# Four of the eleven steps of each feed-forward computed in pairs, by seven block products in place of eight, with the loop unrolled

## The chip, the core and the metric

The kernel runs on one core of one Trainium2 chip. TensorE (PE) multiplies and writes its results to PSUM, in eight banks of 128 partitions x 512 float32. VectorE (DVE), ScalarE (ACT) and GpSimd (POOL) work on SBUF, and DVE and ACT also read PSUM. SyncE (SP) issues the transfers of the weights from the chip's memory. Each engine takes its instructions in order, and they wait for one another through semaphores. The metric is the time of one execution in microseconds (us), lower is better, as the median of several runs.

## What is computed

Two blocks of two layers each, for 256 tokens of width 1024 in float32. Each layer has a mixer (an attention, a gated or a recurrent one) between two feed-forwards, so there are eight feed-forwards in all. The change touches only them. This is the function and its use in the first block; the second block has the same two in each layer:

```python
D_MODEL = 1024
SEQ = 256
DEPTH = 2
D_FF = 2816

def _swiglu(x, w1, w3, w2):
    return (jax.nn.silu(x @ w1) * (x @ w3)) @ w2

    for l in range(DEPTH):
        h = _swiglu(x, ffn_w1[l, 0], ffn_w3[l, 0], ffn_w2[l, 0])
        x = _layernorm(ALPHA * x + 0.5 * h, ln_g[l, 0], ln_b[l, 0])
...
        h = _swiglu(x, ffn_w1[l, 1], ffn_w3[l, 1], ffn_w2[l, 1])
        x = _layernorm(ALPHA * x + 0.5 * h, ln_g[l, 2], ln_b[l, 2])
```

## The kernel before

**Split arithmetic.** Each float32 factor is split into a high part, a rounded copy in the type fp32r, and a low part, what is left of it. A product is three matmuls into one bank (`three`, L1908): high x high (L1909), high x the weights' low (L1910), low x the weights' high (L1911). The weights come into one of six slots: slot s has `wf[s]` (the transfer's target, 128 x 2048 float32, 1 MB), `wh[s]` (high) and `wl[s]` (low). Slots 4 and 5 lie in the area `arena`. For each load ACT makes `wh[s]` with `prep(s)` (L618 to L622; from here a *cast*), which waits for the transfer (`ld`) and until PE is done with the slot (`used`). Then DVE makes `wl[s]` with `low(s)` (L1120; from here a *low*), which waits for the cast (`hi`). SP may load `wf[s]` again when the low has been made (`lo`), and it issues its loads in a fixed order, each after that wait.

**A step.** The 2816 hidden columns are worked in eleven steps of 256. The *up* part of a step multiplies the tokens (`xTh`, `xTl`: eight tiles of 128 along the width, two blocks b of 128 tokens) with 256 columns of w1 and 256 of w3 side by side, 512 columns in all, in two units of 1 MB: unit h = 0 has the first 512 rows of the weights, h = 1 the others. The results of the two token blocks are in banks 4 and 5. That is 2 x 8 x 3 = 48 matmuls of 512 columns. ACT takes the silu of the first half of each bank (`silu`, L631), DVE multiplies it with the second (`gated`, L1139, semaphore `h_ready`). PE turns the 256 x 256 hidden values with four small matmuls into bank 6 (`ht_tr`); ACT and DVE split them into `hTh`, `hTl`. The *down* part multiplies them with 256 rows of w2 (1 MB, one slot) into banks 0 to 3, which add up over all steps: 24 matmuls.

**Order.** Everything is written out by hand. Two steps are done in the head (`skewed_head`, L2016; in the first feed-forward `first_head`, L1985), together with the end of what came before. A loop of eight passes follows (L2045 for PE, L716 for ACT, L1297 for DVE, L381 for SP): PE does the up units of a step from slots 0 and 1, the down part of the step before from slot 2, waits for `h_ready` and turns the step's hidden values. The last step lies in the tail. The down part of the last step is in slot 3, which is loaded at the start of the feed-forward; slots 4 and 5 lie unused through the loop. One pass on DVE, and on PE:

```python
                low(0)
                for b in range(TB):
                    ins = gated(b, 4 + b, half)
                ins.then_inc(SEM["h_ready"], 1)
                low(1)
                dve.wait_ge(SEM["ht_hi"], c.next("ht_hi"))
...
                low(2)
```

`settle` (L1126) lets DVE wait for the end of its own last instruction, where the next one reads what that one wrote. The area `y` (128 x 2 x 1024) is free from the head on until the tail.

## Time and profile before

| | |
|---|---|
| runs (us) | 2439.42, 2439.14, 2440.81 |
| median | 2439.42 |
| span of the profiled execution | 2436.0 |
| PE busy | 2394.2 (98%) |
| DVE busy | 1455.7 (60%) |
| ACT busy | 1070.4 (44%) |
| transfers from the chip's memory | 422.49 MB, 174 GB/s over the span |
| mean granted clock of TensorE | 0.996 |

The profiled execution is one run of its own. Its span goes from the first instruction to the last and lies 3.4 us under the median of the runs; what is outside the span is the same for either kernel as far as the profile tells. Matmuls overlap: one lasts 0.39 us in the profile, but the next begins 0.23 us after it, so sums of PE's durations tell less than its starts.

### The profile page before, as it was taken

The numbers are of one execution on the slowest core, as the hardware profiler recorded it, in microseconds if no ns is written. First come the engines' busy times: TensorE is split into PE (matmuls) and PEld (weight loads), VectorE is DVE, ScalarE is ACT, GpSimd is POOL, SyncE is SP. The second block draws the span as 40 slices with busy tenths as digits, with TensorE's granted clock in tenths as the row PEclk, the third lists the DMA queues.
The fourth block names the chain that finished last, engine by engine and source line by source line (L and its number), as shares of the span: only waits on it lengthen the run. The fifth ranks groups of instructions, "written<-read, shape, count | busy, mean of one in ns | idle before, by whom it ended". The sixth has DMA issues, their size and how long they took to land.

```text
span 2436.0 us, 29857 instructions
## 1 busy us (share of the span) xinstructions
PE 2394.2 (98%) x11668; PEld 1978.8 (81%) x11668; DVE 1455.7 (60%) x1599; ACT 1070.4 (44%) x1308; POOL 119.6 (5%) x145
## 2 busy tenths in 40 slices
PE   9999999999999999999999999999999999999998
PEld 8888877888888888788887887798888888777887
DVE  5456867655654666675456456797555545646544
ACT  4443455343343444554344344534434444545442
POOL 0001000000000000000001002102000000200000
PEclk9999999999999999999999999999999999999999
DMA  8566534565655654455564565204556555334552
GB/s 278 187 217 201 189 105 173 191 194 186 206 177 186 210 197 173 139 190 183 188 224 159 187 218 195 91 1 142 194 186 203 187 187 198 121 139 142 186 189 86
DMA packets 281236, 426.58 MB, mean 175 GB/s; under 512 B 11747, under 2 KB 193635, under 8 KB 281136
## 3 DMA queue, kind: packets, MB, share of 16 engines
q1 hardware_dynamic: 273632, 400.04, 49.4%
q0 software_dynamic: 7520, 25.37, 3.4%
q8 instruction: 59, 0.97, 0.2%
q14 instruction: 25, 0.20, 0.0%
HBM read 422.49 MB, written 1.05 MB: 174 GB/s over the span
## 4 chain that ended last, share of the span: by engine, by line
PE 83%; DVE 12%; ACT 2%; issue 1%; POOL 1%; DMA 0%; SPq 0%; DVEq 0%; POOLq 0%; ACTq 0%
PE bank L1909 25%; PE bank L1911 24%; PE bank L1910 24%; DVE wl L1120 4%; PE bank L2366 2%; PE bank L2056 1%; POOL rstd L463 1%; PE bank L1956 1%; DVE stats L1155 1%; DVE arena L1618 1%; DVE y L1222 1%; DVE x L1164 1%; PE bank L2161 1%; DVE y L1189 1%; DVE x L1225 1%
## 5 line engine op out<-in xcount | busy, mean ns | idle before, releaser
L1120 DVE TENSOR_TENSOR wl<-wf,wh 128x2048 fp32r<-128x2048 f32 x355 | 808.6, 2290 | 420.6 <-ACT wh L622 420.1
L1909 PE MATMUL bank<-wh,xTh 128*128 128x512 f32 x2336 | 926.2, 396 | 13.6 <-DVE wl L1120 7.2
L1911 PE MATMUL bank<-wh,xTl 128*128 128x512 f32 x2336 | 910.3, 390 | 0.0
L1910 PE MATMUL bank<-wl,xTh 128*128 128x512 f32 x2336 | 909.1, 389 | 0.0
L622 ACT ACTIVATE wh<-wf 128x2048 fp32r<-128x2048 f32 x355 | 673.3, 1915 | 243.8 <-PE bank L1911 237.8
L1909 PEld LDWEIGHTS bank<-wh,xTh 128*128 128x128 f32 x2336 | 439.6, 188 | 106.7 <-issue 8.7
L1911 PEld LDWEIGHTS bank<-wh,xTl 128*128 128x128 f32 x2336 | 439.1, 188 | 93.2
L1910 PEld LDWEIGHTS bank<-wl,xTh 128*128 128x128 f32 x2336 | 439.9, 188 | 86.5 <-issue 0.7
L1909 PE MATMUL bank<-wh,hTh 128*128 128x512 f32 x704 | 277.4, 394 | 0.2
L1911 PE MATMUL bank<-wh,hTl 128*128 128x512 f32 x704 | 275.0, 391 | 0.0
L1910 PE MATMUL bank<-wl,hTh 128*128 128x512 f32 x704 | 274.6, 390 | 0.0
L631 ACT ACTIVATE sil<-bank 128x256 f32<-128x256 f32 x176 | 60.4, 381 | 297.5 <-PE bank L1911 297.5
L1911 PEld LDWEIGHTS bank<-wh,hTl 128*128 128x128 f32 x704 | 132.4, 188 | 27.9
L1909 PEld LDWEIGHTS bank<-wh,hTh 128*128 128x128 f32 x704 | 132.5, 188 | 27.2 <-DVE wl L1120 0.6
L1910 PEld LDWEIGHTS bank<-wl,hTh 128*128 128x128 f32 x704 | 132.6, 188 | 26.7
L1139 DVE SCALAR_TENSOR_TENSOR hid<-sil,bank 128x256 f32<-128x256 f32 x176 | 68.2, 418 | 124.7 <-ACT sil L631 124.3
L723 ACT ACTIVATE hTh<-bank 128x512 fp32r<-128x512 f32 x64 | 38.3, 598 | 218.7 <-PE bank L2056 218.7
L463 POOL TENSOR_TENSOR rstd<-ve,mhalf 128x1 f32<-128x1 f32 x42 | 35.8, 853 | 1673.4 <-DVE ve L1159 830.0
L1304 DVE TENSOR_TENSOR hTl<-bank,hTh 128x512 fp32r<-128x512 f32 x64 | 44.3, 692 | 110.3 <-ACT hTh L723 110.3
L627 ACT ACTIVATE xTh<-bank 128x512 fp32r<-128x512 f32 x72 | 39.1, 596 | 81.9 <-PE bank L1956 81.5
L2366 PE MATMUL bank<-wf 128*128 128x128 f32 x544 | 65.5, 280 | 3.3 <-DVE wf L1605 2.5
L2366 PEld LDWEIGHTS bank<-wf 128*128 128x128 f32 x544 | 63.0, 195 | 5.6 <-DVE wf L1605 2.9
(333 smaller groups left out, 1512.4 us busy)
## 6 DMA issues: line engine op xcount, KB each, us to landing
wf<-in_ffn_w SPq DMA_DIRECT2D x160, 512.0 KB, 4.8
wf<-in_w_in SPq DMA_DIRECT2D x52, 1024.0 KB, 5.6
wf<-in_ffn_w SPq DMA_DIRECT2D x44, 1024.0 KB, 5.1
wf<-in_ffn_w_down SPq DMA_DIRECT2D x44, 1024.0 KB, 5.1
wf<-in_ffn_w_gate SPq DMA_DIRECT2D x80, 512.0 KB, 4.0
wf<-in_ffn_w_up SPq DMA_DIRECT2D x80, 512.0 KB, 5.0
wf<-in_w_branch SPq DMA_DIRECT2D x16, 1024.0 KB, 5.2
wf<-in_c_w_in SPq DMA_DIRECT2D x14, 1024.0 KB, 6.4
```

Source lines behind the costliest of these rows:

```text
L463: pool.tensor_tensor(dst, src, mhalf[:, 0:n], ALU.pow).then_inc(SEM[to], 1)
L622: act.activation(wh[s], wf[s], ACT.Copy).then_inc(SEM[f"hi{s}"], 1)
L627: act.activation(xTh[:, 4 * r:4 * r + 4, b * P:(b + 1) * P], bank[banks[r]][:, :].rearrange("p (k t) -> p k t", k=4), ACT.Copy).then_inc(S ...
L631: act.activation(sil[:, b, :], bank[bk][:, 0:STEP], ACT.Silu).then_inc(SEM["h_silu"], 1)
L723: act.activation(hTh[0][:, :, :], bank[6][:, :].rearrange("p (k t) -> p k t", k=2), ACT.Copy)\
L1120: dve.tensor_tensor(wl[s], wf[s], wh[s].bitcast(f32), ALU.subtract).then_inc(SEM[f"lo{s}"], 1)
L1139: return dve.scalar_tensor_tensor(hid[:, b, :], sil[:, b, :], half, bank[bk][:, STEP:2 * STEP], ALU.mult, ALU.mult)
L1304: dve.tensor_tensor(hTl[0][:, :, :], bank[6][:, :].rearrange("p (k t) -> p k t", k=2), hTh[0][:, :, :].bitcast(f32), ALU.subtract).then_in ...
L1909: pe.matmul(o, lh, rh, start=start, stop=False)
L1910: pe.matmul(o, lh, rl, start=False, stop=False)
L1911: return pe.matmul(o, ll, rh, start=False, stop=stop)
L2366: ins = pe.matmul(bank[bk][:, i * P:(i + 1) * P], left[:, i, :], right[:, i, :], start=True, stop=True)
```

## The change

Steps 2 to 9, until now the passes of the loop, become two *bodies* of four steps ja, jb, jc, jd written out (2 to 5 and 6 to 9). In each, ja and jb are computed as before. jc and jd are a pair: their two up products are one product of a matrix A (256 tokens x 1024) with B (1024 x 1024), and both are cut into 2 x 2 blocks: A11, A12 are the first token block's two halves along the width, A21, A22 the second's; B11 is jc's first unit, B21 its second, B12 and B22 those of jd. It is computed in Strassen's manner (Winograd's variant) by seven products of 12 matmuls each (`product`) in place of eight.

- **Sums of A**, once in each feed-forward, in body 0: `block_sums` on DVE, ten instructions of 128 x 512, into `wf[5]`, and a cast and a low for slot 5.
- **Sums of B**, once per pair: four subtractions or additions of 128 x 2048 on DVE (`t_made`), in place in `wf[0]`, `wf[1]`, `wf[4]`, `wf[2]`. Three of the seven right factors are loaded blocks, four are such sums; each has a cast and a low of its own (`cast`, `low_of`).
- **Results**: bank 4 (X) goes on adding up through four products; ACT copies it three times on the way (`snapshot`, semaphore `snap`) to quarters of `y`. DVE adds banks 5 (Y) and 7 (Z) to these copies (`block_of`), and silu and gate work from there (`c_silu`, `c_gated`, four of each as before). PE turns the pair's hidden values into banks 6 and 7 (`blocks_hidden`), after the first unit of the next step.
- **Slots**: ja uses slots 3 and 4 in body 0 (0 and 1 in body 1), jb 3 and 1, the pair 4, 1, 3, 2; down parts are in 2, 0, 4 (or 5), 2. The last step's down is now loaded into slot 3 after everything else.
- The loops and what counted in them go; some semaphores are shared. Nothing else of the kernel moves.

```diff
@@ SP, ffn
-            down(w2, STEPS - 1, 3)
-            with c.loop(STEPS - 2, "sp ffn") as j:
-                up(w1, w3, j + 2, 0)
-                down(w2, j + 1)
+            for i in range(BODIES):
+                ja, jb, jc, jd = range(2 + 4 * i, 6 + 4 * i)
+                if i == 0:
+                    up_unit(w1, w3, ja, 3, 0)
+                    up_unit(w1, w3, ja, 4, 1)
+                    down(w2, 1)
+                up_unit(w1, w3, jb, 3, 0)
+                up_unit(w1, w3, jb, 1, 1)
+                down(w2, ja, 0)
+                up_unit(w1, w3, jc, 4, 0)
+                up_unit(w1, w3, jd, 1, 0, "b12_ld")
+                up_unit(w1, w3, jd, 3, 1, "b22_ld")
+                up_unit(w1, w3, jc, 2, 1)
+                sp.wait_ge(SEM["lo3"], c.so_far("lo3"))
+                down(w2, jb, 4)
...
+                up(w1, w3, jd + 1, 0)
+                down(w2, jc, 4 if i < BODIES - 1 else 5)
+                sp.wait_ge(SEM["lo3"], c.so_far("lo3"))
+                down(w2, jd, 2)
+            down(w2, STEPS - 1, 3)
@@ ACT, ffn
-            prep(3)
-            with c.loop(STEPS - 3, "act ffn"):
-                prep(0, 2)
...
+            for i in range(BODIES):
+                if i == 0:
+                    prep(1, 2)
+                    prep(0)
+                    act.wait_ge(SEM["t_made"], c.next("t_made"))
+                    cast(5, wf[5])
+                    prep(3, 2)
+                    act.wait_ge(SEM["used4"], c.so_far("used4"))
+                    silus()
...
+                prep(4, 2)
+                take_both(1)
+                prep(2, 2)
+                act.wait_ge(SEM["t_made"], c.next("t_made", 3))
+                cast(3, wf[4])
+                act.wait_ge(SEM["used1"], c.so_far("used1"))
+                silus()
+                cast(1, wf[1])
+                cast(0, wf[0])
+                take_both(0)
+                snapshot(part_1, 4)
+                prep(4)
...
@@ DVE
+        def block_sums():
...
+            s1, s2, s3, s4 = (sumA[:, j, :, :] for j in range(4))
+            dve.tensor_tensor(s1, A(1, 0, xTh), A(1, 1, xTh), ALU.add)
+            dve.tensor_tensor(s2, A(1, 0, xTl), A(1, 1, xTl), ALU.add)
+            dve.tensor_tensor(s3, A(0, 0, xTh), A(1, 0, xTh), ALU.subtract)
+            settle(dve.tensor_tensor(s4, A(0, 0, xTl), A(1, 0, xTl), ALU.subtract))
+            dve.tensor_tensor(s1, s1, s2, ALU.add)
+            settle(dve.tensor_tensor(s3, s3, s4, ALU.add))
+            settle(dve.tensor_tensor(s2, s1, A(0, 0, xTh), ALU.subtract))
+            settle(dve.tensor_tensor(s2, s2, A(0, 0, xTl), ALU.subtract))
+            settle(dve.tensor_tensor(s4, A(0, 1, xTh), s2, ALU.subtract))
+            dve.tensor_tensor(s4, s4, A(0, 1, xTl), ALU.add).then_inc(SEM["t_made"], 1)
...
+            for i in range(BODIES):
+                if i == 0:
+                    low(1)
+                    low(0)
+                    block_sums()
+                    low(5)
+                    low(3)
+                    both_gated(half)
+                else:
+                    low(3)
+                    take_both(1)
+                    take_both(0, 7)
+                    low(0)
+                    both_gated(half)
+                    low(1)
+                low(4)
+                dve.wait_ge(SEM["b12_ld"], c.next("b12_ld", 32))
+                dve.tensor_tensor(wf[0], wf[1], wf[4], ALU.subtract).then_inc(SEM["t_made"], 1)
+                dve.wait_ge(SEM["b22_ld"], c.next("b22_ld", 32))
+                dve.tensor_tensor(wf[1], wf[3], wf[1], ALU.subtract).then_inc(SEM["t_made"], 1)
+                take_both(1)
+                dve.wait_ge(SEM["t_made"], c.next("t_made", 2))
+                dve.tensor_tensor(wf[4], wf[1], wf[4], ALU.add).then_inc(SEM["t_made"], 1)
+                low(2)
+                dve.wait_ge(SEM["t_made"], c.next("t_made"))
+                dve.tensor_tensor(wf[2], wf[2], wf[4], ALU.subtract).then_inc(SEM["t_made"], 1)
+                low_of(3, wf[4])
+                both_gated(half)
...
@@ PE, ffn
-            with c.loop(STEPS - 3, "pe ffn"):
-                for h in range(2):
-                    whole_unit(h, h, [bank[4][:, :], bank[5][:, :]])
...
+            for i in range(BODIES):
+                if i == 0:
+                    whole_unit(3, 0, outs45)
+                    whole_unit(4, 1, outs45)
+                    both_down(2, 0)
...
+                pe.wait_ge(SEM["h_ready"], c.next("h_ready"))
+                both_hidden()
+                whole_unit(3, 0, outs45)
+                whole_unit(1, 1, outs45)
+                both_down(0, 1)
+                pe.wait_ge(SEM["h_ready"], c.next("h_ready"))
+                both_hidden()
+                product(4, A(0, 0), bankX, True)
+                product(2, A(0, 1), bankY, True)
...
+                product(3, A_sum(SUM2), bankX, False)
+                product(1, A_sum(SUM3), bankZ, True)
...
+                product(0, A_sum(SUM1), bankX, False)
+                both_down(4, 0)
...
+                product(2, A_sum(SUM4), bankX, False)
...
+                product(3, A(1, 1), bankZ, False, "used5" if i == BODIES - 1 else None)
```

How the order stands at the places that matter, by engine. **DVE, from the last low of the head on**, before (the whole pass of the loop; wl0 is the low of slot 0):

```order
L1120 TENSOR_TENSOR wl0<-wf0,wh0 128x2048 [waits hi0]
L1138 ISA
L1139 SCALAR_TENSOR_TENSOR hid<-sil,bank4 128x256 [waits h_silu]
L1138 REGISTER_ALU
L1139 SCALAR_TENSOR_TENSOR hid<-sil,bank5 128x256 [waits h_silu]
L1120 TENSOR_TENSOR wl1<-wf1,wh1 128x2048 [waits hi1]
L1304 TENSOR_TENSOR hTl<-bank6,hTh 128x512 [waits ht_hi]
L1120 TENSOR_TENSOR wl2<-wf2,wh2 128x2048 [waits hi2]
```

and in the changed kernel, body 0, from the low of the second up unit of jb (wl1) to the gate of ja (`hid`); the five rows left out are more sums:

```order
L1177 TENSOR_TENSOR wl1<-wf1,wh1 128x2048 [waits hi1]
L1177 TENSOR_TENSOR wl0<-wf0,wh0 128x2048 [waits hi0]
L1195 TENSOR_TENSOR arena<-xTh 128x512
L1196 TENSOR_TENSOR arena<-xTl 128x512
L1197 TENSOR_TENSOR arena<-xTh 128x512
...
L1203 TENSOR_TENSOR arena<-xTh,arena 128x512 [waits dve]
L1204 TENSOR_TENSOR arena<-arena,xTl 128x512 [waits dve]
L1177 TENSOR_TENSOR wl5_52<-arena,wh5_51 128x2048 [waits hi5]
L1177 TENSOR_TENSOR wl3<-wf3,wh3 128x2048 [waits hi3]
L1233 SCALAR_TENSOR_TENSOR hid<-sil,bank4 128x256 [waits h_silu]
L1233 SCALAR_TENSOR_TENSOR hid<-sil,bank5 128x256 [waits h_silu]
```

Before, one low stands ahead of a step's gate; now two lows, ten sums and two more lows stand ahead of the first one. **ACT at the same place**, before (one pass) and then in the changed kernel:

```order
L620 REGISTER_ALU [waits ld0]
L622 ACTIVATE wh0<-wf0 128x2048 [waits used0]
L631 ACTIVATE sil<-bank4 128x256 [waits used1]
L631 ACTIVATE sil<-bank5 128x256
L622 ACTIVATE wh1<-wf1 128x2048 [waits used1,ld1]
L723 ACTIVATE hTh<-bank6 128x512 [waits ht_tr]
```

```order
L618 ACTIVATE wh1<-wf1 128x2048 [waits used1,ld1]
L618 ACTIVATE wh0<-wf0 128x2048 [waits used0,ld0]
L629 ACTIVATE wh5_51<-arena 128x2048 [waits used5,t_made]
L618 ACTIVATE wh3<-wf3 128x2048 [waits used3,ld3]
L643 ACTIVATE sil<-bank4 128x256 [waits used4]
L643 ACTIVATE sil<-bank5 128x256
L618 ACTIVATE wh4_49<-arena 128x2048 [waits used4,ld4]
```

The silus of ja now stand behind a cast that waits for the sums. **PE in the pair**, the first row of each group of matmuls (each product goes on for eleven more rows):

```order
L2118 MATMUL bank6<-ident,hid 128x128 [waits h_ready]
...
L2141 MATMUL bank4<-wh4_49,xTh 128x512 [waits lo4]
...
L2141 MATMUL bank5<-wh2,xTh 128x512 [waits lo2]
...
L2141 MATMUL bank4<-wh3,wh5_51 128x512 [waits lo3,lo5,snap]
...
L2141 MATMUL bank7<-wh1,wh5_51 128x512 [waits lo1]
...
L2141 MATMUL bank4<-wh0,wh5_51 128x512 [waits lo0,snap]
...
L2049 MATMUL bank0<-wh4_49,hTh 128x512 [waits lo4,ht_ready]
...
L2141 MATMUL bank4<-wh2,wh5_51 128x512 [waits lo2,snap]
...
L2141 MATMUL bank7<-wh3,xTh 128x512 [waits lo3,c_made]
```

and before, where a pass ends and turns its hidden values:

```order
L1909 MATMUL bank3<-wh2,hTh 128x512
L1910 MATMUL bank3<-wl2,hTh 128x512
L1911 MATMUL bank3<-wh2,hTl 128x512
L2053 REGISTER_ALU
L2056 MATMUL bank6<-ident,hid 128x128 [waits h_ready]
L2056 MATMUL bank6<-ident,hid 128x128 x3
```

The wait for `h_ready` stands at the same distance behind the units as before; the pair has one wait for a copy, or for DVE's results, at nearly every product.

## Rows read from the trace of the kernel before

**Rows 1.** The page: busy time of each engine, then the chain by engine.
```profile
PE 2394.2 (98%) x11668; PEld 1978.8 (81%) x11668; DVE 1455.7 (60%) x1599; ACT 1070.4 (44%) x1308; POOL 119.6 (5%) x145
...
PE 83%; DVE 12%; ACT 2%; issue 1%; POOL 1%; DMA 0%; SPq 0%; DVEq 0%; POOLq 0%; ACTq 0%
```

**Rows 2.** PE in order of time (start us, us): matmuls of a head, then two passes' turns.
```profile
486.06 0.39 PE L1910 MATMUL bank<-wl,xTh 128*128 128x512 f32 x1
486.29 0.40 PE L1911 MATMUL bank<-wh,xTl 128*128 128x512 f32 x1
...
607.34 0.60 PE L2056 MATMUL bank<-ident,hid 128*128 128x128 f32 x4
624.13 0.60 PE L2056 MATMUL bank<-ident,hid 128*128 128x128 f32 x4
```

**Rows 3.** The page, groups of instructions: busy us, mean ns of one, idle before.
```profile
L1120 DVE TENSOR_TENSOR wl<-wf,wh 128x2048 fp32r<-128x2048 f32 x355 | 808.6, 2290 | 420.6 <-ACT wh L622 420.1
...
L622 ACT ACTIVATE wh<-wf 128x2048 fp32r<-128x2048 f32 x355 | 673.3, 1915 | 243.8 <-PE bank L1911 237.8
...
L723 ACT ACTIVATE hTh<-bank 128x512 fp32r<-128x512 f32 x64 | 38.3, 598 | 218.7 <-PE bank L2056 218.7
...
L1304 DVE TENSOR_TENSOR hTl<-bank,hTh 128x512 fp32r<-128x512 f32 x64 | 44.3, 692 | 110.3 <-ACT hTh L723 110.3
```

**Rows 4.** Second feed-forward, end of the head: DVE, ACT, PE; then PE's turns (source view).
```profile
486.86 2.29 DVE L1120 TENSOR_TENSOR wl<-wf,wh 128x2048 fp32r<-128x2048 f32 x1 [1.38 <-ACT wh L622]
...
484.91 1.91 ACT L622 ACTIVATE wh<-wf 128x2048 fp32r<-128x2048 f32 x1
490.63 1.91 ACT L622 ACTIVATE wh<-wf 128x2048 fp32r<-128x2048 f32 x1
...
489.93 0.38 PE L1963 MATMUL bank<-ident,hid 128*128 128x128 f32 x2
...
L2056 PE MATMUL bank<-ident,hid x24: 270/272/273, 506.5 to 590.9; 128*128 128x128 f32 x24
```

**Rows 5.** First feed-forward, end of the head: DVE, PE; then PE's turns (source view).
```profile
30.56 0.41 DVE L1139 SCALAR_TENSOR_TENSOR hid<-sil,bank 128x256 f32<-128x256 f32 x1
...
40.58 0.60 PE L1978 MATMUL bank<-ident,hid 128*128 128x128 f32 x4
...
L2056 PE MATMUL bank<-ident,hid x32: 269/272/273, 57.4 to 175.3; 128*128 128x128 f32 x32
```

**Rows 6.** Transfers: issue to landing (page); a full stretch (windows: busy of engines, clock, share, GB/s).
```profile
wf<-in_ffn_w SPq DMA_DIRECT2D x160, 512.0 KB, 4.8
...
16.00:18.00 2.00, 2.00 (x10) 1.65 (x10) 1.60 (x1) 1.64 (x1) 0.00 (x0) 1.00 1.11 357
```

**Rows 7.** DVE on 128 x 512: a group by form, then two in time, the last waiting.
```profile
L1609 DVE TENSOR_TENSOR wf<-wf,ident 128x512 f32<-128x512 f32 x4 | 2.6, 686 | 0.0
...
461.89 1.28 DVE L1155 BATCH_NORM_STATS2 stats<-y 128x6 f32<-128x512 f32 x2
463.33 0.21 DVE L1158 BATCH_NORM_AGGREGATE mv<-stats 128x2 f32<-128x12 f32 x1 [0.16 <-DVE stats L1155]
```

**Rows 8.** A gap of PE: windows (PE, PEld, DVE, ACT, POOL, clock, share, GB/s), and the end.
```profile
1564.00:1565.00 1.00, 0.00 (x0) 0.00 (x0) 1.00 (x3) 0.53 (x2) 0.00 (x0) 1.00 0.00 0
1565.00:1566.00 1.00, 0.28 (x2) 0.28 (x3) 1.00 (x3) 0.00 (x0) 0.00 (x0) 1.00 0.00 0
1566.00:1567.00 1.00, 1.00 (x8) 1.00 (x8) 0.86 (x2) 0.00 (x0) 0.00 (x0) 0.64 0.00 0
1567.00:1568.00 1.00, 1.00 (x7) 1.00 (x7) 0.55 (x1) 0.00 (x0) 0.00 (x0) 0.50 0.00 0
1568.00:1569.00 1.00, 1.00 (x6) 1.00 (x6) 0.14 (x1) 0.00 (x0) 0.00 (x0) 0.50 0.00 0
1569.00:1570.00 1.00, 1.00 (x8) 1.00 (x7) 0.94 (x2) 0.12 (x1) 0.00 (x0) 0.66 0.00 0
...
2430.00:2431.00 1.00, 0.00 (x0) 0.00 (x0) 0.99 (x2) 0.00 (x0) 0.00 (x0) 0.50 0.00 0
```

More of the change, by code:

```diff
@@ L12 @@
 import math
-from contextlib import ExitStack, contextmanager
+from contextlib import ExitStack
 import numpy as np
@@ L210, in program @@
     negm = negm_wide[:, P:T]
+    yq = [y[:, i // 2, (i % 2) * HALF:(i % 2 + 1) * HALF] for i in range(4)]
+    C11, C21, C12, C22 = yq
+    part_v, part_1, part_5 = C21, C12, C22
+    sumA = wf[5].rearrange("p (j k t) -> p j k t", j=4, k=4)
+    sumA_h, sumA_l = (t[5].rearrange("p (j k t) -> p j k t", j=4, k=4) for t in (wh, wl))
+    SUM1, SUM2, SUM3, SUM4 = range(4)
+    bankX, bankY, bankZ = (bank[i][:, :] for i in (4, 5, 7))
     names = []
@@ L342, in _, with load @@
         c = Counts(sp, SEM["held"])
-        def load(s, *pieces):
+        def load(s, *pieces, to=None):
             sp.wait_ge(SEM[f"lo{s}"], c.so_far(f"lo{s}"))
@@ L628, in take_x, with cast, snapshot, c_silu @@
                                bank[banks[r]][:, :].rearrange("p (k t) -> p k t", k=4), ACT.Copy).then_inc(SEM["xt_hi"], 1)
+        def cast(s, src):
+            act.wait_ge(SEM[f"used{s}"], c.so_far(f"used{s}"))
+            c.count(f"used{s}")
+            act.activation(wh[s], src, ACT.Copy).then_inc(SEM[f"hi{s}"], 1)
+        def snapshot(to, s):
+            act.wait_ge(SEM[f"used{s}"], c.so_far(f"used{s}"))
+            act.activation(to, bankX, ACT.Copy).then_inc(SEM["snap"], 1)
+        def c_silu(to, src):
+            act.activation(to[:, 0:STEP], src[:, 0:STEP], ACT.Silu).then_inc(SEM["h_silu"], 1)
+        def silus():
+            for b in range(TB):
+                silu(b, 4 + b)
         def silu(b, bk):
@@ L726, in ffn @@
+            prep(2)
+            take_both(1)
+            take_both(0, 7)
+            prep(3)
             if after:
@@ L1307, in ffn @@
+            low(5)
+            take_both(1)
+            take_both(0, 7)
+            low(2)
+            low(3)
             gated(0, 4, half).then_inc(SEM["h_ready"], 1)
@@ L1979, in both_hidden, with both_down, A, A_sum @@
             ins.then_inc(SEM["ht_tr"], 1)
+        outs45 = [bank[4][:, :], bank[5][:, :]]
+        def both_down(s, i):
+            pe.wait_ge(SEM["ht_ready"], c.next("ht_ready"))
+            pe.wait_ge(SEM[f"lo{s}"], c.next(f"lo{s}"))
+            for b in range(TB):
+                ins = down(s, i, b, (0, 1))
+            ins.then_inc(SEM[f"used{s}"], 1)
+        def A(b, r):
+            t = slice(b * P, (b + 1) * P)
+            return [(xTh[:, 4 * r + q, t], xTl[:, 4 * r + q, t]) for q in range(4)]
+        def A_sum(j):
+            return [(sumA_h[:, j, q, :], sumA_l[:, j, q, :]) for q in range(4)]
+        def product(s, lhs, o, start, freed=None):
+            pe.wait_ge(SEM[f"lo{s}"], c.next(f"lo{s}"))
+            for q, (lh, ll) in enumerate(lhs):
+                r = slice(q * HALF, (q + 1) * HALF)
+                ins = pe.matmul(o, lh, wh[s][:, r], start=start and q == 0, stop=False, skip_group_check=not start)
+                if freed and q == 0:
+                    ins.then_inc(SEM[freed], 1)
+                pe.matmul(o, lh, wl[s][:, r], start=False, stop=False, skip_group_check=not start)
+                ins = pe.matmul(o, ll, wh[s][:, r], start=False, stop=q == 3, skip_group_check=not start)
+            ins.then_inc(SEM[f"used{s}"], 1)
+        def blocks_read():
+            pe.wait_ge(SEM["h_ready"], c.next("h_ready", 3))
+        def blocks_hidden():
+            pe.wait_ge(SEM["h_ready"], c.next("h_ready"))
+            for rows_, bk in (((C11, C21), 6), ((C12, C22), 7)):
+                for k in range(2):
+                    for b in range(TB):
+                        ins = pe.transpose(bank[bk][:, k * T + b * P:k * T + (b + 1) * P], rows_[b][:, k * P:(k + 1) * P],
+                                           ident[:, :])
+                ins.then_inc(SEM["ht_tr"], 1)
         def busy(n, bk, t):
@@ L2061, in ffn @@
+            blocks_read()
+            unit(0, 0, 0, bank[4][:, :])
+            blocks_hidden()
+            unit(1, 1, 0, bank[4][:, :]).then_inc(SEM["up"], 1)
+            both_down(5, 1)
             pe.wait_ge(SEM["ht_ready"], c.next("ht_ready"))
```

214 lines of the change are left out of this document (129 added, 85 removed), and 5 rows, old and new, of the table PER_PASS.

## The prediction

> **What bounds the kernel now.** I read the page first: PE is busy 98% of the span, DVE 60%, ACT 44%, and 83% of the chain that ended last is PE's own work [rows 1]. Then PE in order of time: matmuls of 512 columns start 0.23 us apart and a pass of the loop comes every 16.79 us (607.34 to 624.13) [rows 2]. The second feed-forward has its loop begin at 490.2 (after the head's last two turns at 489.93) and turns its first hidden values at 506.5 [rows 4]: 16.3 us for 72 matmuls, 0.227 us each, so PE has no hole there. Each matmul taken out of a pass is worth 0.227 us, as long as the others keep up. DVE's slack in a pass: three lows of 2.29 and about 1.4 us of small work, 8.3 of 16.8 us. That is an average; where a change piles work in front of one PE wait, the average says nothing. So the sum needs the order on DVE and ACT, walked through with these durations.
>
> **What goes from PE.** A pair needs 84 up matmuls in place of 96. Two pairs in eight feed-forwards: 16 x 12 = 192 matmuls x 0.227 = **43.6 us** less. The down matmuls and the turns are as many as before. The loop cost PE nothing that a row shows (16.79 = 72 x 0.227 + four turns at about 0.11), so its unrolling gives nothing.
>
> **What comes on DVE and ACT, per pair.** DVE: three more lows (seven right factors in place of four units) and four sums of 128 x 2048, at 2.29 each [rows 3] = 16.0, and three `block_of` at 0.69: +18. ACT: three more casts at 1.92 and three copies at 0.60 [rows 3]: +7.6. Over a body of four steps (PE: 4 x 16.8 - 2.7 = 64.4) DVE then needs about 4 x 8.3 + 18 = 51 and ACT about 37. On average both fit.
>
> **What comes on DVE once per feed-forward, in body 0.** Ten sums of 128 x 512. The nearest rows: 0.69 alone, 0.60 from start to start in a row (1.28 for two), and 0.16 of idle before an instruction that waits for the one before it [rows 7]. Five are settled (0.69 + 0.16), four follow freely (0.60), the last takes 0.69: 4.25 + 2.4 + 0.69 = 7.3 us. Bounds: 6.0 (all at 0.60) to 8.5 (all settled). On the wait inside such a chain the Trainium skill ("VectorE: DVE Perf Modes", The DRAIN you can't avoid) says that a semaphore after each instruction costs nothing extra; the 0.16 us of rows 7 speak against it. By its rule the sums would take 10 x 0.69 = 6.9 us and the total 3 us less.
>
> **The place that decides: the first turn of body 0.** PE does ja's two units (48 matmuls) and a down part (24), 16.3 us, then waits for ja's gated values. On DVE that gate stands behind: low of slot 4, low 2, low 1 (jb), low 0 (ja's down part), ten sums, low 5, low 3, in this order; on ACT its silus stand behind cast 5, which waits for the sums, and cast 3. Walk for the second feed-forward, body start at 490.2:
> - SP issues jb's first unit (slot 3) when the head's low of that slot is done, 486.86 + 2.29 = 489.15 (before, slot 0; now the same instruction for slot 3) [rows 4], then slot 1 and slot 0 at once, whose buffers are free. A unit is two transfers, the second is issued 0.4 us after the first and lands 4.8 us later [rows 6]: 489.2 + 5.3 = 494.5. The next megabytes queue behind it; at full rate the stream runs at 357 GB/s [rows 6], some 3.0 us for 1 MB: slot 1 lands at 497.5, slot 0 at 500.5.
> - ACT is done with its head casts at 494.5 (490.63 + 2 x 1.92) [rows 4]. Cast 1 497.5 to 499.4, cast 0 500.5 to 502.5.
> - DVE: low 1 to 501.8, low 0 502.5 to 504.8, sums to 512.1. Cast 5 to 514.1, cast 3 to 516.0, silus to 516.7; low 5 514.1 to 516.4, low 3 to 518.7, two gates (0.41 each, 0.75 the overlapping pair) [rows 5] to 519.4.
> - PE, ready at 506.5, turns at 519.5: **it stands 13.0 us**.
>
> With transfers at no cost DVE alone (lows 4, 2, 1, 0 from 492.6 on, sums, wait for cast 5, lows 5 and 3, gates) still ends at 516.5, so 10 us is the lower bound; loads 1 us later make it 14. The first feed-forward loads earlier: its head's slot-3 low may follow the gate at 30.56 as soon as ACT has made the cast, about 34.6, in place of waiting for PE. PE's body starts at 41.0 (turn at 40.58) and would turn at 57.4 [rows 5]. Slots 3, 1, 0 land at 40.0, 43.0, 46.0; the same walk gives low 1 to 48.3, low 0 to 50.6, sums to 57.9, gates to 65.3: 8.0 us. All others begin like the second. Sum: 7 x 13.0 + 8.0 = **99 us** of PE standing.
>
> **After that.** ACT and DVE come out of it late; the next sums of B, which need jd's second unit in slot 3 (loaded only after the late low 3), push low 3 and the gate of jb to 0.8 us behind PE: 8 x 0.8 = 6. From there on the same walk finds no PE wait: in the pair the copies of X take 0.6 us beside the 2.7 of a product into another bank, each right factor's low is done 2 us or more ahead, and in body 1 DVE stands idle ahead of each gate. The tightest place of body 1 is again jb's gate ahead of the pair: done 1.2 us before PE wants it, behind three loads in a row (b12, b22, B21). I take 0 there; loads 1 us slower, or 2 us of extra DVE work, would make it up to 2 us per feed-forward. The tail has DVE's four pieces (low 5, hidden values, lows 2 and 3) 1 us or more ahead, and slot 5's later load lands 20 us before the next head wants it: 0.
>
> **The clock.** PE does nothing from 1564 to 1565 and for 0.72 us of the next window; in the four windows after that the granted clock is 0.64, 0.50, 0.50, 0.66, and it is 0.50 at 2430 too, where PE has no more work [rows 8]. 0.50 is its lower level, 1.2 GHz. The four windows lose 0.36 + 0.50 + 0.50 + 0.34 = 1.7 us. Each of the eight stops is far longer than that gap (1.7 us by the windows), so I charge 1.7 each; between 0 and 3.4 are the bounds. It takes the place of the 0.8 above (PE is later, DVE is not), so 0.9 more: 8 x 0.9 = **7 us**. The Trainium skill ("TensorE: Matmul & The Clock Gate", What's actually happening) says the same in kind, an idle array falls to 1.2 GHz and comes back when kept busy; rows 8 agree with it.
>
> **The sum.** -43.6 + 99 + 6 + 7 = +69 us on the profiled span: 2436.0 + 69 = 2505. The runs' median is 3.4 us over that span, which the change doesn't touch: **2508 us**.
>
> **Rivals.**
> 1. *All of it is hidden, the product saving stays.* It would need the gate of ja 13 us earlier. The order has no room for that: ja's gate stands behind the sums and two more lows on an engine that doesn't reorder, and behind cast 5 on ACT. 2439.4 - 43.6 = **2396**. Against it every row of the walk; for it only that I may have misread which wait is meant. 3%.
> 2. *The stop is real but short*: the transfers are early, the sums near 6.0, the clock unharmed: 10.0 - 1.3 = 8.7 in seven, 5 in the first, 0.8 behind each: +66 + 6 - 44 = +28 to +45: **2467 to 2485**. For it: the landings are the softest numbers of the walk (a lone unit's landing is measured, a burst's is worked out). Against it: DVE's own chain. 12%. At this end, if the change also gained something in the loop that I don't see (over 28 us, 1.8 per pair), it would be no change; 2% for within 0.2%.
> 3. *The pair is too dense as well*: per body 13 pieces of 2.29 us have to come in the right order, and the seven waits of PE in the pair each catch a late low, or the three loads ahead of it come 1 to 2 us late. 2 to 3 us in each of 16 pairs eats the saving: +32 to +48: **2540 to 2556**. For it: the 1.2 us of slack in body 1. Against it: 13 us of standing lets all that is queued behind catch up, and in body 1 DVE waits for casts, not the other way. 10%.
> 4. *The change doesn't do what it says on PE*: a product that adds up in one bank for twelve matmuls runs slower than a unit that changes banks every three. But the matmuls at 486.06 and 486.29 [rows 2] are from a head's unit that stays in bank 5 for twelve, and they stand 0.23 us apart as well. I give it 1%, inside case 3.
>
> **How the numbers follow.** Forecast (a stop of 11.5 to 14.5 in each body 0, saving as counted, clock 0 to 3.4 each): 72%, 2508, own range 2488 to 2530. Case 2: 12%, case 3: 11%, case 1: 3%, no change: 2%. To hold 8 in 10 the range takes the forecast's own and reaches into both neighbours: 2478 to 2534. A measurement of this kernel can tell about 0.2% (5 us) from no change. Slower by more: 0.72 + 0.12 + 0.11 = 0.95, of which 0.02 go to the other two for what the walk may have overlooked: 0.93; within 0.2%: 0.02 + 0.01 = 0.03; faster: 0.03 + 0.01 = 0.04.
>
> **What the profile after would show.** PE's idle ahead of the first turn of each feed-forward after the head, released by DVE's gate: 12 to 14 us, seven times, and about 8 in the first. The 40 slices would show eight dents of PE, with a lower clock in them. In body 1 and in the pairs, PE matmuls 0.227 us apart with no gap over 1 us. PE starts 192 matmuls fewer. DVE busy up by 16 x 18 + 8 x 9.6 = some 365 us, to about 75% of the span. Wrong would be: a stop under 10 us (then the burst of loads or the sums were mis-sized), gaps inside the pairs (case 3), or no stop at all.

## The result, and the profile after

The changed kernel takes **2501.21 us** (median of four runs, 2500.56 to 2504.1), where the one before takes 2439.47 on the same footing: a ratio of 1.0256, with a 95% interval of 1.0243 to 1.027. The profiled execution has a span of 2502.2 us against 2436.0, so 66.2 us have to be explained. Some 3 of them are scatter: the profiled execution is the slowest of the four (2504.1), the other three took 2500.56 to 2501.22. An execution takes 1.8 to 1.9 us longer than its own span, in both kernels (2504.1 for a span of 2502.2, and 2437.8 for one of 2436.0 in the runs of e1). So of the 3.4 us between span and median, only 1.8 lie outside the span; the rest is the distance of that one execution from the median. The page of the changed kernel (busy times; then PE's busy tenths and the granted clock in 40 slices; the chain by engine; and one of the groups):

```profile
PE 2367.5 (95%) x11476; PEld 1954.6 (78%) x11476; DVE 1789.8 (72%) x1847; ACT 1199.7 (48%) x1412; POOL 120.6 (5%) x145
...
PE   8999999989989999998998999999799899999798
...
PEclk9999999989989999998999999999899899999899
...
PE 73%; DVE 17%; ACT 4%; DMA 3%; issue 2%; POOL 1%; SPq 1%; DVEq 0%; POOLq 0%; ACTq 0%
...
L2118 PE MATMUL bank<-ident,hid 128*128 128x128 f32 x136 | 24.5, 310 | 91.6 <-DVE hid L1233 91.6
```

Beside [rows 1]: PE has 192 matmuls fewer (11668 to 11476), and yet less of the span is its own work, 95% for 98%. PE's slices are dented where they were whole, and so is the clock. In the chain 10 points have gone from PE to the other engines. L2118 is the turn of the hidden values: PE stood 91.6 us ahead of it in all, and DVE's gate (L1233) ended the wait. The waits of PE by line say in how many pieces (us, times, longest):

```profile
PE bank L2118 <- DVE hid L1233: 91.6, 8, 12.7
PE bank L2049 <- DVE wl L1177: 7.4, 13, 1.0
PE bank L2103 <- DVE hid L1233: 7.2, 9, 2.4
```

Eight stops, one in each feed-forward; the next two rows were there before, within 0.2 us. These are PE's rows at three of the eight (start, us, and in brackets the idle time ahead), with the three matmuls behind the second:

```profile
64.71 1.12 PE L2118 MATMUL bank<-ident,hid 128*128 128x128 f32 x4 [6.98 <-DVE hid L1233]
...
522.79 1.12 PE L2118 MATMUL bank<-ident,hid 128*128 128x128 f32 x4 [11.74 <-DVE hid L1233]
523.56 0.78 PE L2049 MATMUL bank<-wh,xTh 128*128 128x512 f32 x1
524.13 0.63 PE L2050 MATMUL bank<-wl,xTh 128*128 128x512 f32 x1
524.56 0.63 PE L2051 MATMUL bank<-wh,xTl 128*128 128x512 f32 x1
...
2356.80 1.12 PE L2118 MATMUL bank<-ident,hid 128*128 128x128 f32 x4 [12.75 <-DVE hid L1233]
```

Matmuls of 512 columns start 0.43 us apart behind a stop, not 0.23 as in [rows 2]: the clock is down. In windows around the second stop (length, then busy of PE, PEld, DVE, ACT, POOL, then the granted clock; the last two columns are the transfers):

```profile
512.00:514.00 2.00, 0.00 (x0) 0.00 (x0) 1.93 (x4) 0.00 (x0) 0.00 (x0) 0.79 0.04 14
514.00:516.00 2.00, 0.00 (x0) 0.00 (x0) 1.54 (x3) 0.36 (x1) 0.00 (x0) 0.50 0.00 0
516.00:522.00 6.00, 0.00 (x0) 0.00 (x0) 4.42 (x3) 5.69 (x5) 0.00 (x0) 0.50 0.00 0
522.00:526.00 4.00, 3.21 (x10) 2.74 (x11) 4.00 (x5) 0.60 (x1) 0.00 (x0) 0.50 0.67 199
526.00:527.00 1.00, 1.00 (x5) 0.76 (x4) 1.00 (x1) 0.00 (x0) 0.00 (x0) 0.60 1.09 366
527.00:530.00 3.00, 3.00 (x15) 2.45 (x14) 2.66 (x3) 0.00 (x0) 0.00 (x0) 1.00 0.99 312
```

From 522.8 to 526 PE works at 0.50, in the next window at 0.60, which is some 2.0 us of work lost. Summed in the same way over all windows of 1 us (PE's busy time times what the clock lacks of 1), the kernel before loses 6.8 us, the changed one 25.0, of which 18.2 lie behind the eight stops (1.5 to 3.0 each). So the 66.2 us are **91.6 (stops) - 43.6 (192 matmuls at 0.227) + 18.2 (clock)**. PE's other waits add up to 1.0 us more than before, so the sum closes to about 1 us.

Why the gate is late can be read from DVE and ACT in the second feed-forward. Its body begins at 494.57 here, by the walk's own measure: 0.27 us after the head's last turns, which are at 494.30 (before, 489.93 and 490.2). ACT's casts of slots 1 and 0 and of the sums, then DVE: the lows of slots 1 and 0, the first and the last sum, the lows of slots 5 and 3, the two gates:

```profile
502.14 1.92 ACT L618 ACTIVATE wh<-wf 128x2048 fp32r<-128x2048 f32 x1 [3.43 <-DMA wf<-in_ffn_w]
504.72 1.92 ACT L618 ACTIVATE wh<-wf 128x2048 fp32r<-128x2048 f32 x1 [0.67 <-DMA wf<-in_ffn_w]
...
515.64 1.91 ACT L629 ACTIVATE wh<-arena 128x2048 fp32r<-128x2048 f32 x1 [8.99 <-DVE arena L1204]
...
504.09 2.29 DVE L1177 TENSOR_TENSOR wl<-wf,wh 128x2048 fp32r<-128x2048 f32 x1 [2.66 <-ACT wh L618]
506.68 2.29 DVE L1177 TENSOR_TENSOR wl<-wf,wh 128x2048 fp32r<-128x2048 f32 x1 [0.29 <-ACT wh L618]
508.88 0.68 DVE L1195 TENSOR_TENSOR arena<-xTh 128x512 f32<-128x512 f32 x1
...
514.19 0.69 DVE L1203 TENSOR_TENSOR arena<-xTh,arena 128x512 f32<-128x512 f32 x1
514.91 0.69 DVE L1204 TENSOR_TENSOR arena<-arena,xTl 128x512 f32<-128x512 f32 x1
517.58 2.29 DVE L1177 TENSOR_TENSOR wl<-arena,wh 128x2048 fp32r<-128x2048 f32 x1 [1.97 <-ACT wh L629]
519.79 2.28 DVE L1177 TENSOR_TENSOR wl<-wf,wh 128x2048 fp32r<-128x2048 f32 x1
521.99 0.74 DVE L1233 SCALAR_TENSOR_TENSOR hid<-sil,bank 128x256 f32<-128x256 f32 x2
```

It is a chain with little idle time in it: a landing, two lows, the sums (508.88 to 515.60), the cast of the sums, two lows, the gates. PE's last matmul before the turn starts at 510.66, and the gates end at 522.73.

### The profile page after: what moved, and what is told of

Read it like the earlier page. It is cut to its first block, busy times and chain, and to the rows that moved or that the text cites. A ratio compares the mean times of both kernels' runs of the same rounds, so it can differ in the third digit from the quotient of the medians.

```text
span 2502.2 us, 27918 instructions
## 1 busy us (share of the span) xinstructions
PE 2367.5 (95%) x11476; PEld 1954.6 (78%) x11476; DVE 1789.8 (72%) x1847; ACT 1199.7 (48%) x1412; POOL 120.6 (5%) x145
## 4 chain that ended last, share of the span: by engine, by line
PE 73%; DVE 17%; ACT 4%; DMA 3%; issue 2%; POOL 1%; SPq 1%; DVEq 0%; POOLq 0%; ACTq 0%
PE bank L2049 17%; PE bank L2051 17%; PE bank L2050 17%; DVE wl L1177 7%; PE bank L2145 4%; PE bank L2141 4%; PE bank L2144 4%; PE bank L2568 2%; ACT wh L618 2%; DMA wf<-in_ffn_w_down 2%; DMA wf<-in_ffn_w 1%; POOL rstd L459 1%; PE bank L2096 1%; PE bank L2118 1%; DVE stats L1249 1%
## 5 line engine op out<-in xcount | busy, mean ns | idle before, releaser
L2049 PE MATMUL bank<-wh,xTh 128*128 128x512 f32 x1824 | 730.5, 401 | 13.9 <-DVE wl L1177 7.4
L2051 PE MATMUL bank<-wh,xTl 128*128 128x512 f32 x1824 | 715.6, 392 | 0.0
L2050 PE MATMUL bank<-wl,xTh 128*128 128x512 f32 x1824 | 715.2, 392 | 0.0
L2049 PEld LDWEIGHTS bank<-wh,xTh 128*128 128x128 f32 x1824 | 347.9, 191 | 89.7 <-issue 9.1
L2051 PEld LDWEIGHTS bank<-wh,xTl 128*128 128x128 f32 x1824 | 346.5, 190 | 73.9
L2050 PEld LDWEIGHTS bank<-wl,xTh 128*128 128x128 f32 x1824 | 347.5, 191 | 68.6 <-issue 0.7
L1177 DVE TENSOR_TENSOR wl<-arena,wh 128x2048 fp32r<-128x2048 f32 x87 | 198.2, 2286 | 51.1 <-ACT wh L618 35.3
L618 ACT ACTIVATE wh<-arena 128x2048 fp32r<-128x2048 f32 x79 | 151.0, 1913 | 38.6 <-PE bank L2051 32.2
L1183 DVE TENSOR_TENSOR wl<-wf,wh 128x2048 fp32r<-128x2048 f32 x64 | 145.0, 2285 | 23.9 <-ACT wh L629 23.9
L2118 PE MATMUL bank<-ident,hid 128*128 128x128 f32 x136 | 24.5, 310 | 91.6 <-DVE hid L1233 91.6
L2144 PE MATMUL bank<-wl,wh 128*128 128x512 f32 x256 | 99.6, 389 | 0.0
L2145 PE MATMUL bank<-wh,wl 128*128 128x512 f32 x256 | 99.6, 389 | 0.0
```

The lines of the kernel that those rows point to most:

```text
L618: act.activation(wh[s], wf[s], ACT.Copy).then_inc(SEM[f"hi{s}"], 1)
L1177: dve.tensor_tensor(wl[s], wf[s], wh[s].bitcast(f32), ALU.subtract).then_inc(SEM[f"lo{s}"], 1)
L1183: dve.tensor_tensor(wl[s], src, wh[s].bitcast(f32), ALU.subtract).then_inc(SEM[f"lo{s}"], 1)
L2049: pe.matmul(o, lh, rh, start=start, stop=False)
L2050: pe.matmul(o, lh, rl, start=False, stop=False)
L2051: return pe.matmul(o, ll, rh, start=False, stop=stop)
```

## The experiments

The theory (A): the stops come from the amount and the order of the work on DVE between the head and the first gate, with the late landings ahead of it; the pairs themselves cost nothing. The rivals: the loss lies in the unrolled code; in the pairs; in the transfers alone; or in the order alone.

### e1: the kernel before with its loops written out

```diff
-            with c.loop(STEPS - 3, "pe ffn"):
+            for j in range(STEPS - 3):
```
(and the same on SP, ACT and DVE)

> The kernel before with its loops in the feed-forwards written out and nothing else changed. Theory (the loss is the stop in body 0, the unrolling is free): 2439 +- 2 us, PE's first turn after the head at the same place as before. Rival (the written-out code itself costs, by instructions that have to be fetched or by lost pacing): clearly above 2439, a good part of the 62 us.

Measured: 2440.11 us, ratio 1.0006 (0.9997 to 1.0015). The unrolling costs nothing that can be told: the interval ends at 0.15%, 3.7 us.

### e2: nine of the ten sums left out

The kernel leaves the sums out to see what they cost; its result isn't that of the product.

```diff
-            dve.tensor_tensor(s1, A(1, 0, xTh), A(1, 1, xTh), ALU.add)
...
-            dve.tensor_tensor(s4, s4, A(0, 1, xTl), ALU.add).then_inc(SEM["t_made"], 1)
+            dve.tensor_tensor(s4, A(0, 1, xTh), A(0, 1, xTl), ALU.add).then_inc(SEM["t_made"], 1)
```

> The changed kernel with one of the ten sums of A left (the other nine are left out, so the sums of A are not those of the product). Theory (DVE's chain ahead of ja's gate sets the stop): the sums take 0.7 us in place of the 6.7 of the profile, the stop falls from 11.5 to about 5.5 us, the total by 8 x 6.0 = 48 to 2453 us. Rival (the landing of the loads or ACT sets it): less than 10 us change.

Measured: 2453.54 us, ratio 1.0062 (1.0047 to 1.0077). PE's waits:

```profile
PE bank L2109 <- DVE hid L1224: 43.8, 9, 6.8
```

The stops shrink by 91.6 - 43.8 = 47.8 us, 6.0 in each feed-forward, and nine sums take 508.88 to 514.91, 6.0 us: the sums stand on PE's path with their whole length. What is left is two lows and a cast too many, and the landings.

### e3: small matmuls in the stop, to hold the clock

```diff
                     both_down(2, 0)
+                    busy(95 if ready else 60, 7, ident[:, :])
```

> The changed kernel with 95 small matmuls (60 in the first feed-forward) of the identity into bank 7 ahead of the first turn of body 0, inside PE's stop: 95 x 0.114 = 10.8 us of 11.5 to 12.7. They change no result. Theory (the lower clock after the stop costs about 2.3 us each, 18 us in all): the granted clock stays at 1.00 and the total falls by 15 to 18 us, to about 2485. Rival (the clock costs nothing since DVE sets the pace then as well; the 18 us are gaps elsewhere): 2501, no change.

Measured: 2558.85 us, ratio 1.0491 (1.0475 to 1.0507). A miss: I had taken 0.114 us for one call, but each float32 matmul of 128 columns leaves two records of PE and takes some 0.22. PE's records of the 95 calls in the second feed-forward (source view: minimum, median, maximum ns, first and last start):

```profile
L2162 PE MATMUL bank<-ident x190: 271/275/276, 516.5 to 537.6; 128*128 128x128 f32 x190
```

21.1 us of filler where the stop had 11.7, so the time says nothing by itself. The account does. The eight runs of filler keep PE for 160.6 us, 69.0 more than the stops, and PE's wait at this turn (L2118) is gone; the clock loses 11.9 us in all, 13.1 less than in the changed kernel. That makes +55.9, and the profiled span is 56.4 longer (2558.6): here the 13.1 us of clock did come out in the time. e8 repeats it with half the number.

### e4: the loads of slots 1 and 0 ahead of slot 3

```diff
+                    up_unit(w1, w3, jb, 1, 1)
+                    down(w2, ja, 0)
+                    up_unit(w1, w3, jb, 3, 0)
+                else:
+                    up_unit(w1, w3, jb, 3, 0)
+                    up_unit(w1, w3, jb, 1, 1)
+                    down(w2, ja, 0)
```

> The changed kernel with the loads of jb's second unit (slot 1) and of ja's down part (slot 0) issued ahead of jb's first unit (slot 3) in body 0, so that they don't wait for the head's low of slot 3. Theory (the burst of three loads holds DVE's first two lows back by some 3 us): the stop falls by 3.0 us in seven feed-forwards and not in the first, 2480 us. Rival (the landings are hidden by DVE's own chain): no change, 2501; or the landings matter all the more and the stop goes.

Measured: 2478.87 us, ratio 1.0169 (1.0153 to 1.0184).

```profile
PE bank L2122 <- DVE hid L1237: 67.3, 9, 8.6
```

```profile
63.66 1.11 PE L2122 MATMUL bank<-ident,hid 128*128 128x128 f32 x4 [6.64 <-DVE hid L1237]
```

The stops shrink by 24.3 us. The first goes from 6.98 to 6.64 (the row shown), as expected, and the other seven, 11.57 to 12.75 before, are now all 8.62 or 8.63: 2.9 to 4.1 less, 3.5 in the mean, where I had taken the 3.0 of one megabyte of the stream. That the seven are now alike points to the landings as the source of their spread. So the landings and DVE's chain are in series. Of the 61.7 us that the changed kernel is slower by, the order of the loads is 22.

### e5: the same work in another order, the gate first

```diff
@@ DVE, body 0
+                    low(3)
                     low(1)
                     low(0)
+                    both_gated(half)
                     block_sums()
+                    low(4)
                     low(5)
-                    low(3)
-                    both_gated(half)
```
(ACT's casts and silus in the same order)

> The changed kernel with another order in body 0, the same work: casts and lows 3, 1, 0, then ja's silus and gates, then the ten sums, lows 4 and 5. Theory A (it is the amount of DVE work ahead of the pair that stops PE, not only its order): no stop at the first turn, but about 4.9 us ahead of ja's down part (its hidden values are split behind the sums) and 4.5 ahead of the next turn, 9.4 in place of 11.5; with the clock's price once or twice 2484 to 2500 us. Theory B (the order alone is at fault): both stops and the clock's price go, 2391 to 2400 us.

Measured: 2466.3 us, ratio 1.0113 (1.0096 to 1.013). It lies under the 2484 to 2500 of the theory and far over the 2391 to 2400 of its rival. PE's first gate is on time now, and two later rows wait, ja's down part for the low half of its hidden values (`hTl`) and jb's turn for its gate:

```profile
PE bank L2051 <- DVE hTl L1332: 28.9, 8, 4.4
PE bank L2120 <- DVE hid L1234: 17.9, 8, 3.7
```

46.8 us in all, 5.9 in each feed-forward. The theory wanted 9.4, the rival that only the order counts wanted none. In the second feed-forward DVE has no idle time from 502.16 to 532.8: jb's gate ends at 532.84 because everything ahead of it is work. So with the sums kept in body 0 the order is worth 45 us of the stops, and the amount of work there the other 47; e6 and e10 move that work instead. Two shorter gaps cost the clock more than one long one: 30.7 us lost in all, 23.9 over the kernel before, for 18.2 in the changed kernel.

### e6: the sums moved into the head

```diff
@@ DVE, skewed_head
             gated(0, 5, half).then_inc(SEM["h_ready"], 1)
             take_x(1)
+            block_sums()
             take_hidden(0, 0)
...
             gated(1, 5, half).then_inc(SEM["h_ready"], 1)
+            low(5)
@@ DVE, body 0
+                    low(3)
+                    low(0)
                     low(1)
-                    low(0)
-                    block_sums()
-                    low(5)
-                    low(3)
                     both_gated(half)
```
(with the cast of slot 5 in ACT's head, the first head likewise, the loads in the order 3, 0, 1, and one `settle` more among the sums, six for five)

> The changed kernel with the sums of A made in the head, in DVE's idle time behind the split of the second token block, their cast and low in the head too; in body 0 the casts and lows 3, 0, 1 and then ja's gates. Theory: no stop at the first turn, about 2.9 us ahead of the turn of jb's hidden values in body 0 (the sums of B stand ahead of the gate); 7 to 8 such stops: 2410 to 2425 us, faster than before the change. Rival (the pairs are too dense for DVE and ACT even so): stops in both bodies, 2440 or more.

Measured: 2432.46 us, ratio 0.9975 (0.9965 to 0.9984). The first stop is gone in all eight feed-forwards, and the head, where [rows 4] shows DVE idle ahead of its lows, takes the sums without a wait of PE. What is left is the gate of jb:

```profile
PE bank L2126 <- DVE hid L1239: 24.4, 8, 3.7
```

-43.6 + 24.4 + 7.6 (clock, 14.4 less 6.8) = -11.6, and the span is 10.2 under that of before. The median is 7 us above the 2410 to 2425 that I expected. The waits are as expected (24.4 for 7 to 8 of 2.9), and the clock, for which I had left little room, is most of the rest of the excess: 7.6 us in the profiled execution, and more in the others. That one is the fastest of ten (2427.7, mean granted clock 0.993); the others have 0.988 to 0.991, and the slowest, 2436.65, has the lowest.

### e7: e6, with the gate of jb ahead of the last sum of B and of the cast and the low of `wf[4]`

```diff
@@ DVE, both bodies
                 low(2)
+                both_gated(half)
                 dve.wait_ge(SEM["t_made"], c.next("t_made"))
                 dve.tensor_tensor(wf[2], wf[2], wf[4], ALU.subtract).then_inc(SEM["t_made"], 1)
                 low_of(3, wf[4])
-                both_gated(half)
```
(ACT's silus ahead of `cast(3, wf[4])`)

> As the one before, and in both bodies jb's silus and gates ahead of the cast of the second sum and of the fourth sum of B. Theory: the 2.9 us go, at most 1.7 us ahead of one product in body 0 are left: 2398 to 2412 us; the product saving of 43.6 us comes out, less 2 to 15. Rival: the same as the one before, since ACT gets the silus no earlier.

Measured: 2410.74 us, ratio 0.9884 (0.9867 to 0.990), near the upper end of what I expected. One row of waits is new, PE's third product into bank 4 waiting for ACT's copy of X; ACT and then PE in order of time show why:

```profile
PE bank L2149 <- ACT y L637: 10.6, 8, 1.8
```
```profile
529.58 1.92 ACT L622 ACTIVATE wh<-arena 128x2048 fp32r<-128x2048 f32 x1 [3.94 <-DMA arena<-in_ffn_w]
531.41 0.40 ACT L640 ACTIVATE y<-y 128x256 f32<-128x256 f32 x1
531.71 1.90 ACT L633 ACTIVATE wh<-wf 128x2048 fp32r<-128x2048 f32 x1
533.51 0.57 ACT L637 ACTIVATE y<-bank 128x512 f32<-128x512 f32 x1
...
534.14 0.50 PE L2149 MATMUL bank<-wh,wh 128*128 128x512 f32 x1 [0.98 <-ACT y L637]
```

ACT waits for the load of slot 4, and the copy (L637) stands behind the cast of that load, a silu and another cast.

### e8: e3 with half the fillers

```diff
-                    busy(95 if ready else 60, 7, ident[:, :])
+                    busy(48 if ready else 26, 7, ident[:, :])
```

> As e3, with 48 matmuls (26 in the first feed-forward) in place of 95 and 60, since one of them turned out to take 0.226 us, not 0.114: 10.8 and 5.9 us, shorter than each stop. Theory (the lower clock after the eight stops costs 18.2 us): the clock stays at its upper level in the feed-forwards and the total falls by 15 to 18 us against the changed kernel, 2483 to 2486 us. Rival (it costs nothing): 2501 us.

Measured: 2500.41 us, ratio 1.0246 (1.0229 to 1.0264), 0.8 us under the changed kernel: the rival's number, not the theory's. The four runs lie far apart (2495.04 to 2503.41). PE's waits, and its rows in the second feed-forward:

```profile
PE bank L2118 <- DVE hid L1233: 19.0, 15, 2.5
```
```profile
510.66 10.88 PE L2162 MATMUL bank<-ident 128*128 128x128 f32 x96
524.03 0.66 PE L2118 MATMUL bank<-ident,hid 128*128 128x128 f32 x4 [2.49 <-DVE hid L1233]
541.30 0.66 PE L2118 MATMUL bank<-ident,hid 128*128 128x128 f32 x4 [0.26 <-DVE hid L1233]
```

The clock lost behind the stops is back, but for 1.7 us behind the last one: 10.2 us are lost in all, in place of 25.0, a gain of 14.8. Most of it didn't show in the time. Against the changed kernel seven second stops appear, at the gate of jb, 5.9 us together; the first stops (fillers 80.8, waits 13.1) are 2.3 us longer; 2.4 us stand in no row that I found; the profiled span is 4.2 us less. The second stops are the prediction's own 0.8 each: in the changed kernel DVE's gates of jb run from 539.09 to 539.83 and PE turns at 541.53; without the 2.0 us that the clock took it would have been ready at 539.5, and stood 0.3, as it does here (0.26). Of the 2.3 us 1.5 are in the second feed-forward, with later landings (the cast of slot 1 starts at 503.33, with its load issued 0.2 us earlier than in the changed kernel); why they land later I can't tell.

### e9: e7, with the cast and the low of slot 4 one place later

```diff
@@ ACT
                 snapshot(part_1, 4)
-                prep(4)
...
                 snapshot(part_v, 3)
+                prep(4)
```
(and `low(4)` behind `low_of(2, wf[3])` on DVE)

> As e7, and in the pair the cast and the low of jb's down part (slot 4) one place later: behind the second copy of X on ACT, behind the low of B22 on DVE. Theory: the wait of PE for that copy, 10.6 us in all in e7's profile, comes from ACT standing in front of a late load; it goes: 2400 +- 3 us, the counted saving of 43.6 us less some clock. Rival: the wait moves to the down part of jb or to the next low, no change against 2411 us.

Measured: 2410.57 us, ratio 0.9877 (0.9861 to 0.9894): no better than e7, the rival's number. The wait for the copy has gone down to 1.4 us, and the down part's for the low of slot 4 has come up by as much:

```profile
PE bank L2057 <- DVE wl L1183: 16.6, 21, 1.2
...
PE bank L2149 <- ACT y L637: 1.4, 4, 0.5
```

In e7 the first row was 7.5 us in 13 times. I had moved a piece that two consumers needed, where it was enough to move the one that was in the way.

### e10: e7, with the copy of X right behind the cast of slot 4

```diff
@@ ACT
                 prep(4)
+                snapshot(part_v, 3)
                 act.wait_ge(SEM["c_made"], c.next("c_made"))
                 c_silu(C11, C11)
                 act.wait_ge(SEM["b22_ld"], c.next("b22_ld", 32))
                 cast(2, wf[3])
-                snapshot(part_v, 3)
```

> As e7_gate_jb, but ACT's second copy of X (the snapshot into part_v) stands right behind the cast of slot 4, ahead of the silu of C11 and of the cast of D22 (in e7_gate_jb it stood behind both). In e7_gate_jb the second feed-forward's cast of slot 4 ends at 531.5, the silu and the cast follow to 533.6, the copy ends at 534.1, and PE, ready at 533.15, waits 0.98 us; 10.6 us in eight waits. e9_snap moved the cast of slot 4 down and the wait went to the low of slot 4. Theory A (only the copy's place was wrong; the cast of slot 4 fits where it is): the copy is made at 531.4 to 532.0, 1.1 us ahead of PE, the low of slot 4 stays at 531.5 to 533.8, 1.6 us ahead of its down part; the cast of D22 comes 0.5 later, its low ends at 536.5, PE wants it at 538. All eight waits go: 2410.7 - 10.6 = 2400 us, within 2398 to 2404. Theory B (ACT and DVE have no place left in this pair): the wait comes back at another row, as in e9_snap, and the time stays at 2408 to 2412.

Measured: **2399.94 us** (2399.71 to 2400.22), ratio 0.9836 (0.9819 to 0.9852). ACT at the same place as in e7, the copy now in the second row; then the page and the first rows of PE's waits:

```profile
527.68 1.92 ACT L622 ACTIVATE wh<-arena 128x2048 fp32r<-128x2048 f32 x1 [3.81 <-DMA arena<-in_ffn_w]
529.50 0.57 ACT L637 ACTIVATE y<-bank 128x512 f32<-128x512 f32 x1
529.98 0.41 ACT L640 ACTIVATE y<-y 128x256 f32<-128x256 f32 x1
530.28 3.71 ACT L633 ACTIVATE wh<-wf 128x2048 fp32r<-128x2048 f32 x2
```
```profile
PE 2354.1 (98%) x11476; PEld 1943.8 (81%) x11476; DVE 1788.2 (75%) x1847; ACT 1200.0 (50%) x1412; POOL 120.6 (5%) x145
```
```profile
PE bank L2057 <- DVE wl L1183: 7.5, 13, 1.0
PE bank L2111 <- DVE hid L1239: 7.2, 9, 2.4
```

Of the waits of PE in the feed-forwards that the kernel before didn't have, 0.9 us is left, in three pieces of 0.24 to 0.38, for the gates of a pair. The span is 37.7 us under that of before: 43.6 for the matmuls, less 3.4 of clock (10.2 less 6.8), those 0.9, and 1.3 at the very start of the program, for the transfer of x; 0.3 is left. The same seven products, sums and casts, with as many instructions on each engine as in the changed kernel (11476, 1847, 1412), make 2501 or 2400 us by their order.

## Why the prediction was right

**The place and the mechanism**: right. PE stands once in each feed-forward, at the first turn of body 0, released by DVE's gate; e2, e4 and e5 show the sums, the landings and the order as its parts, e6 that it is gone when the sums and low 5 are made in the head and the loads come in the order 3, 0, 1.

**The size of the stop**: 99 us forecast (seven of 13.0, one of 8.0), 91.6 measured (11.57 to 12.75, and 6.98). From the start of the body in the second feed-forward the walk said: sums from +14.6 to +21.9, gates done at +29.2. They were at +14.3, +21.0 and +28.2. So 0.3 is the landings and lows, 0.6 the sums, 0.2 the cast and lows behind them, and PE itself was ready 0.2 us later: 13.0 less 1.3 is the 11.7 measured. Four of the seven are under the 12 that I had given as a sign, none under 11.5.

The sums took 6.7 us for 7.3. The 0.16 us of idle that [rows 7] had shown on a short instruction did not add itself to the 0.69 of these: a sum that waits for its neighbour starts 0.72 us after it (514.19 to 514.91), one that doesn't 0.60. The rule weighed there (the Trainium skill, "VectorE: DVE Perf Modes", The DRAIN you can't avoid: a semaphore behind each instruction costs nothing extra) came nearer to the chain's length, 6.9 us by it. That is luck: 5 x 0.72 + 4 x 0.60 + 0.69 is the 6.7 measured, and ten times 0.69 takes the five that wait too short and the four that don't too long. The trace has 0.12 between a sum that waits and one that doesn't, so between 128 x 512 pieces the wait isn't free.

**The second stop**: 6 us forecast beside 7 of clock; neither came in that form. The profile shows no second stop, and 18.2 us of lost clock. The term that was mis-sized is the clock's: I took the 1.7 us of a short gap [rows 8] for each, between 0 and 3.4, and it was 1.5 to 3.0, 2.3 in the mean. The 0.8 us that I took off for the second stop was right in kind, as e8 shows, where PE at the full clock stands at jb's turn seven times for 5.9 us. The two misses, -7.4 for the stops and +5.2 for the rest (18.2 against 13), cancel to 2.2 us, which is why 2505 for the span stood so near to 2502.2: the closeness is luck, the mechanism isn't. The forecast of the runs, 2508 for 2501.21, was further off by the 3.4 us that I put on the span: the span of the profiled execution, the slowest of four, lies 1.0 us over the median. The Trainium skill's rule on the clock ("TensorE: Matmul & The Clock Gate", What's actually happening) was borne out in kind: idle, the array fell to 0.50 (1.2 GHz), and it came back when it was busy again.

**The saving on PE**: right. 192 records fewer, 0.227 us each; the accounts of e2, e4 and e10 close within 0.5 us with it.

**Unrolling, the pairs, body 1, the tail at nothing**: right. e1 says so for the unrolling, and e10 for the others: it keeps both pairs and PE stands 0.9 us for them in all. The rival of pairs that are too dense falls for the changed kernel. It had a point all the same, hidden by the long stop: as soon as the stop goes, jb's gate (e6, 24.4 us) and the second copy (e7, 10.6 us) come up one after the other.

**DVE's load**: 365 us more forecast, 334.1 measured (1789.8 less 1455.7), since DVE's pieces in a row overlap and the busy time counts that once: a low takes 2.29 us and the next starts 2.20 after it (517.58, 519.79, 521.99).

**The rival that all is hidden**, 2396 us: rightly given little for this order. As an account of what the products can give it was within 4 us of e10.

## What to carry to other kernels

A saving on the engine that sets the pace is kept only if what it costs the others is spread over places where they have air: an average load of 60% on DVE says nothing about fourteen pieces put in front of one wait. Walk the order of each engine to the first thing that the bounding engine waits for, and put sums that need only the layer's input where that engine idles, here the head. Then go on wait by wait: each one mended shows the next, and it is mended by moving the piece that is in the way, not the one that is needed twice.
